# The last pair's up products ahead of the down products of the last pair but one, in two expert stages

## The reference

```python
xn = rms_norm(x)
group = argmax(xn @ w_router_group + b_router_group)
two experts = top_2 of the logits of that group       # weights e_w
for each expert e, on the tokens that chose it:
    hid = silu(xn @ w1[e]) * (xn @ w3[e])             # gate and up: 1024 x 512 each
    y   = hid @ w2[e]                                 # down: 512 x 1024
x = x + sum over a token's two experts of e_w * y
```

## Time and profile before

| | us |
|---|---|
| median of 3 runs | 2242.19 (2239.77 to 2244.62) |
| the profiled execution | 2242.67 |
| its span | 2240.8 |
| TensorE busy | 2118.8 (95%) |
| VectorE busy | 733.4 (33%) |
| ScalarE busy | 387.8 (17%) |
| GpSimd busy | 245.4 (11%) |
| bytes moved | 528.81 MB, mean 236 GB/s |

### The profile page before, as it was taken

How to read it: one execution, slowest core, us unless ns; L and a number is a source line. 1 busy time by engine, 2 the same in 40 slices (tenths; PEclk the granted TensorE clock), 3 DMA queues, 4 the chain that set the end, 5 groups by cost and what they waited for, 6 DMA issues and landing times.

```text
span 2240.8 us, 27584 instructions
## 1 busy us (share of the span) xinstructions
PE 2118.8 (95%) x11803; PEld 1130.3 (50%) x11803; DVE 733.4 (33%) x1742; ACT 387.8 (17%) x742; POOL 245.4 (11%) x258
## 2 busy tenths in 40 slices
PE   9999899999998999989999999999999999998987
PEld 5454666654444433335556568764674533333332
DVE  3126675323001011041277864522232411111104
ACT  4001132121000100011133353210022100000001
POOL 6001211000000000000001142301110010000001
PEclk9999999999999999999998999999999999999999
DMA  8113104259999999995110021124352699999998
GB/s 300 50 38 113 50 26 169 83 208 389 424 422 428 427 421 427 428 391 179 29 30 2 3 77 39 64 87 150 113 225 94 237 421 427 428 428 427 427 425 334
DMA packets 96686, 528.81 MB, mean 236 GB/s; under 512 B 10286, under 2 KB 26339, under 8 KB 69162
## 3 DMA queue, kind: packets, MB, share of 16 engines
q1 hardware_dynamic: 82450, 492.11, 54.1%
q0 software_dynamic: 8160, 17.88, 2.2%
q10 hardware_dynamic: 5944, 16.94, 2.0%
HBM read 509.04 MB, written 30.41 MB: 241 GB/s over the span
## 4 chain that ended last, share of the span: by engine, by line
PE 79%; DMA 11%; DVE 5%; SPq 2%; ACT 1%; issue 1%; POOL 0%; DVEq 0%; POOLq 0%; ACTq 0%
PE ps L204 75%; DMA SC<-in_w_e_up 2%; DMA RING<-in_w_e_up 2%; DMA SC<-in_w_e_down 2%; SPq L1688 2%; DMA SC<-in_w 1%; DMA XT<-in_w 1%; DMA EX<-in_w_e_up 1%; DMA RING<-in_w 1%; PE ps L1774 1%; ACT SC L1931 1%; PE ps L1822 1%; PE ps L3349 0%; PE ps L2754 0%; DVE RING L3420 0%
## 5 line engine op out<-in xcount | busy, mean ns | idle before, releaser
L204 PE MATMUL ps<-SC 64*64 64x64 f32 (+5 forms) x5408 | 743.9, 348 | 46.7 <-ACT SC L1931 11.0
L204 PE MATMUL ps<-RING,SC 128*64 128x512 f32 (+2 forms) x1648 | 558.6, 587 | 22.7 <-ACT SC L1931 5.5
L204 PEld LDWEIGHTS ps<-SC 64*64 64x64 f32 (+2 forms) x5408 | 331.4, 146 | 343.9 <-issue 292.4
L204 PEld LDWEIGHTS ps<-RING,SC 128*64 128x64 f32 (+2 forms) x1648 | 192.6, 151 | 256.1 <-issue 245.5
L204 PE MATMUL ps<-XT,RING 128*128 128x256 f32 (+2 forms) x944 | 317.1, 489 | 3.0 <-DVE XT L200 1.6
L204 PEld LDWEIGHTS ps<-XT,RING 128*128 128x128 f32 (+1 forms) x944 | 176.2, 190 | 115.6 <-issue 100.4
L1999 DVE SCALAR_TENSOR_TENSOR SC<-ps,ST,SC 128x512 f32<-128x512 f32 x30 | 22.5, 751 | 643.2 <-PE ps L204 643.2
L204 PE MATMUL ps<-RING,XT 128*128 128x512 f32 (+1 forms) x384 | 147.8, 545 | 0.0
L204 PE MATMUL ps<-SC,RING 128*128 128x512 f32 (+2 forms) x504 | 134.6, 432 | 2.3 <-DVE SC L1270 0.8
L204 PE MATMUL ps<-XT,SC 128*64 128x512 f32 (+2 forms) x312 | 117.1, 528 | 2.0 <-DMA SC<-in_w_e_up 1.3
L204 PEld LDWEIGHTS ps<-RING,XT 128*128 128x128 f32 x384 | 69.5, 195 | 76.5 <-issue 75.8
(11 more groups left out here) (497 smaller groups left out, 1950.9 us busy)
## 6 DMA issues: line engine op xcount, KB each, us to landing
SC<-in_w SPq DMA_DIRECT2D x48, 2048.0 KB, 29.1
RING<-in_w SPq DMA_DIRECT2D x36, 2048.0 KB, 28.9
RING<-in_w_in SPq DMA_DIRECT2D x15, 2048.0 KB, 9.1
SC<-in_w_e_gate SPq DMA_DIRECT2D x14, 2048.0 KB, 40.9
SC<-in_w_e_up SPq DMA_DIRECT2D x13, 2048.0 KB, 41.7
SC<-in_w_e_down SPq DMA_DIRECT2D x13, 2048.0 KB, 37.5
RING<-in_w_e_gate SPq DMA_DIRECT2D x11, 2048.0 KB, 40.4
RING<-in_w_e_up SPq DMA_DIRECT2D x11, 2048.0 KB, 42.2
```

Of the source, the lines that this page charges most:

```text
L204: return e.matmul(out, l, r, start=st, stop=sp, skip_group_check=True)
```

## The change

SP's order of loads is now: pairs 0 to 13 as they were, gate and up of pair 14, gate and up of pair 15, down of pair 14, down of pair 15. The down weights of pair 14 come as column halves too, and before them SP waits for the first halves of the last gate weights (the two share a semaphore). `down_p` and `down_a` are split into the transposition (`ht_p`, `ht_a`) and the products; for pair 15 the transposition comes first, then pair 14's down products, then pair 15's. ScalarE's copy of HT for pair 15 waits for the end of pair 14's down products. Pair 15's down result goes to XG in place of YS, both halves by ScalarE. VectorE makes the one-hots after the last gate product.

```diff
--- before.py
+++ after.py
@@ -1687,33 +1687,38 @@
                         k = dst.shape[1] // 2
                         e.dma_start(dst[:, k * hf:k * hf + k], src[:, k * hf:k * hf + k]).then_inc(*(up or slots.up)(label))
 
-            put_n = 0
-            while put_n < 6 * NPAIR:
+            turn = list(range(6 * LAST - 2)) + [6 * LAST + i for i in (0, 1, 2, 3, -2, -1, 4, 5)]
+            i_ = 0
+            while i_ < 6 * NPAIR:
+                put_n = turn[i_]
                 if put_n == 2 and bi == 0:
                     mk_s(e)
                 if bi == 0 and put_n in MV_LOADS:
                     mv_s(e, 1 - MV_LOADS.index(put_n))
                 if put_n == nfirst:
                     halves(([c.on("half of w", 0, 0)], None), ([], None))
-                    put_n += 2
+                    i_ += 2
                 elif put_n in (6 * LAST, 6 * LAST + 2):
                     j = put_n // 2 % 3
                     halves(([], lambda label: c.up(f"dh{j}", "half", LAST, j)), ([], None))
-                    put_n += 2
-                elif put_n == 6 * LAST + 4:
+                    i_ += 2
+                elif put_n in (6 * LAST - 2, 6 * LAST + 4):
+                    p_ = put_n // 6
                     loads = [put(n) for n in (put_n, put_n + 1)]
+                    if p_ < LAST:
+                        W.wait_ge(*c.on("half", LAST, 0))
                     for hf in range(2):
                         for label, free, dst, src in loads:
                             for f in () if hf else free:
                                 W.wait_ge(*f)
-                            e.dma_start(dst[:, :, 512 * hf:512 * hf + 512], src[:, :, 512 * hf:512 * hf + 512]).then_inc(*(slots.up(label) if hf else c.up("dh2", "half", LAST, 2)))
-                    put_n += 2
+                            e.dma_start(dst[:, :, 512 * hf:512 * hf + 512], src[:, :, 512 * hf:512 * hf + 512]).then_inc(*(slots.up(label) if hf else c.up("dh2" if p_ == LAST else "dh0", "half", p_, 2)))
+                    i_ += 2
                 else:
                     label, free, dst, src = put(put_n)
                     for f in free:
                         W.wait_ge(*f)
                     e.dma_start(dst, src).then_inc(*slots.up(label))
-                    put_n += 1
+                    i_ += 1
             slots.put(hots_at, ("hot", bi), (c, ("add", NT - 1, 1)))
             for i in ybs:
                 for f in slots.put(i, ("yb", bi, i), (c, ("X", NT - 1)))[1]:
@@ -1814,13 +1819,15 @@
                     i = mm(e, b[:, :], hotp[tt], X[:, tt, 512 * hf:512 * hf + 512], tt == 0, tt == NT - 1)
                 i.then_inc(*c.up("p", "pick", q, hf))
 
-        def down_p(e, f, q, banks, w):
+        def ht_p(e, f, q, banks):
             b, free = banks("ht", q)
             W.wait_ge(*free)
             W.wait_ge(*f.on("hd", q))
             for j in range(4):
                 i = e.transpose(b[:, j * 128:(j + 1) * 128], HD.rearrange("p (c k) -> p k c", k=4)[:, j, :], ident[:, :])
             i.then_inc(*f.up("p", "ht", q))
+
+        def down_p(e, f, q, banks, w):
             W.wait_ge(*f.on("ev", "ht", q))
             for hf in range(2):
                 wv = w(q, 2, hf)
@@ -1841,7 +1848,7 @@
             for tt in range(NT):
                 b, free = c.take("add", tt, hf)
                 W.wait_ge(*free)
-                i = mm(e, b[:, :], hot2[:, tt * 128:(tt + 1) * 128], YS[:, hf * 512:(hf + 1) * 512], True, tt != 3)
+                i = mm(e, b[:, :], hot2[:, tt * 128:(tt + 1) * 128], XG[:, hf * 512:(hf + 1) * 512], True, tt != 3)
                 if tt < 3:
                     i.then_inc(*c.up("p", "add", tt, hf))
             if hf:
@@ -1866,7 +1873,7 @@
             def w(q, j, hf):
 
                 labels = [(f"m{bi}", q, j, x) for x in range(2)]
-                if q == LAST and not hf:
+                if not hf and (q == LAST or (q, j) == (LAST - 1, 2)):
                     W.wait_ge(*c.on("half", q, j))
                 else:
                     for l in labels:
@@ -1886,7 +1893,11 @@
                     for tt in range(NT):
                         i = e.transpose(b[:, tt * 128:(tt + 1) * 128], hot[:, tt * 128:(tt + 1) * 128], ident[:, :])
                     i.then_inc(*c.up("p", "hot T"))
-                down_p(e, c, q, c.take, w)
+                ht_p(e, c, q, c.take)
+                if q == LAST:
+                    down_p(e, c, LAST - 1, c.take, w)
+                if q != LAST - 1:
+                    down_p(e, c, q, c.take, w)
                 if q == 0:
                     turn_e(e, c, 1, c.take)
                 if bi == 0 and q in MV_AFTER:
@@ -1908,6 +1919,7 @@
             def pair_p(q):
                 turn_e(e, o, q, banks)
                 up_p(e, o, q, banks, ow)
+                ht_p(e, o, q, banks)
                 down_p(e, o, q, banks, ow)
 
             segments(e, over(e), pair_p)
@@ -1924,16 +1936,22 @@
                 W.wait_ge(*c.on("rsl"))
                 e.activation(HD, at("up", q, 0)[:, :], AF.Silu, scale=rsl[:, i_:i_ + 1]).then_inc(*f.up("a", "ev", "up", q, 0))
 
-        def down_a(e, f, q, at):
+        def ht_a(e, f, q, at):
             W.wait_ge(*f.on("ht", q))
             if f is c and q == 0:
                 W.wait_ge(*c.on("nov"))
+            if f is c and q == LAST:
+                W.wait_ge(*f.on("down", q - 1, 1))
             e.activation(HT, at("ht", q)[:, :], AF.Copy).then_inc(*f.up("a", "ev", "ht", q))
+
+        def down_a(e, f, q, at):
+            if f is c and q == LAST:
+                for hf in range(2):
+                    W.wait_ge(*f.on("down", q, hf))
+                    e.activation(XG[:, 512 * hf:512 * hf + 512], at("down", q, hf)[:, :], AF.Copy).then_inc(*f.up("a", "ev", "down", q, hf))
+                return
             if q >= 1 and f is c:
                 W.wait_ge(*f.on("y", q - 1))
-            if q == LAST and f is c:
-                W.wait_ge(*f.on("down", q, 0))
-                e.activation(YS[:, 0:512], at("down", q, 0)[:, :], AF.Copy).then_inc(*f.up("a", "ev", "down", q, 0))
             W.wait_ge(*f.on("down", q, 1))
             e.activation(YS[:, 512:1024], at("down", q, 1)[:, :], AF.Copy).then_inc(*f.up("a", "ev", "down", q, 1))
 
@@ -1960,7 +1978,11 @@
                 if q == LAST:
                     W.wait_ge(*c.on("hot T"))
                     e.activation(hot2, c.at("hot")[:, :], AF.Copy).then_inc(*c.up("a", "ev", "hot"))
-                down_a(e, c, q, c.at)
+                ht_a(e, c, q, c.at)
+                if q == LAST:
+                    down_a(e, c, LAST - 1, c.at)
+                if q != LAST - 1:
+                    down_a(e, c, q, c.at)
                 if bi == 0 and q in MV_AFTER:
                     for n in range(4):
                         mv_a(e, c, 1 - MV_AFTER.index(q), n)
@@ -1970,6 +1992,7 @@
 
             def pair_a(q):
                 up_a(e, o, q, fixed_at)
+                ht_a(e, o, q, fixed_at)
                 down_a(e, o, q, fixed_at)
 
             def table():
@@ -2308,9 +2331,11 @@
                 turn_v_(e, c, q + 1, c.at)
                 if q + 2 in picks:
                     hotp_v(e, q + 2)
-                down_v(e, c, q, c.at)
+                if q < LAST - 1:
+                    down_v(e, c, q, c.at)
             hots_v(e)
             up_v(e, c, LAST, c.at)
+            down_v(e, c, LAST - 1, c.at)
             n_over = over(e)
             for kind, tt, hf in (("add", 0, 0), ("add", 1, 0), ("add", 2, 0), ("table", 0, 0), ("table", 1, 0), ("add", 0, 1), ("add", 1, 1),
                                  ("table", 2, 0), ("add", 2, 1), ("add", 3, 0), ("add", 3, 1)):
@@ -2360,7 +2385,7 @@
 
         def hots_v(e):
 
-            W.wait_ge(*c.on("w", LAST - 1, 2))
+            W.wait_ge(*c.on("w", LAST, 0))
             W.wait_ge(*c.last("v"))
             for k, dst in ((0, hot), (1, hot2)):
                 for tt in range(NT):
```

## The result

The changed kernel takes 2250.6 us (median of 10 runs, 2247.2 to 2259.0), the one before 2242.8 beside it. The ratio is 1.0040 with a 95% interval of 1.0029 to 1.0051, which is 9.0 us more (6.5 to 11.4); the two medians as such are 7.8 us apart, inside that interval. A second measurement gave 1.0037 (1.0024 to 1.0050). The forecast was 2254 in a range of 2247 to 2261. The profiled execution took 2252.8 us with a span of 2251.1.

What follows compares the result with a forecast made beforehand. Weight streams bound both expert stages up to the last landing, with a tail behind. Profiled 2242.67 us plus 6.5 (second stage) and 5.5 (first) gave 2254.7, less 0.5 for the median 2254.2, say 2254; range 2247 to 2261.

Steps and rivals of the forecast that it cites:

- Place and sign: Expert stage tails: down 14, scatter, ytab reads and table passes come to stand in series; slower, chance 0.85.
- (c): Stage tails: the reads of ytab are hidden after all and TensorE's tail stays level, 2242 us; chance 0.03.
- (d): TensorE, not the bytes, is the bound and the order cures its stalls: 3.9 us a stage, 2234.5; chance 0.05.
- Loads: Down 14's column halves move at 389 instead of 421 GB/s, +0.8 us; they land at about 2201.4 and 2206.8.
- Scatter: Pair 14's scatter, second stage, starts at 2212.7 after down 14 and ScalarE's copies, takes 7.8 us, lands at 2220.5.
- Rival (a): Without the stream the scatter lands in 4.7 us: +2 to +3.5 us a stage, 2246 to 2249; chance 0.18.
- the row of 512 KB written by ACT: Nearest row without load for the scatter's landing: 3.7 us, with POOL's 1.0 us 4.7 us.
- Reads: Four ytab reads sent at 2220.5 into an empty queue: 4.8 us for the first, 2.5 more for each, to 2232.8.
- The row of memV: The 1024 KB row used to price the first ytab read in an empty queue: 4.8 us.
- Clock: Second stage: after 4.6 us idle TensorE runs its last eight records at half clock, 1.5 us added.
- Sum: Second stage 6.5 us and first stage 5.5 us longer, added to 2242.67 us: 2254.7, by the median 2254.
- ck1's place: First stage: ck1, 2 MiB queued behind the reads, lands at 1009.3; key products +4.2 to +6.5 us, 5.5 taken.

Runs made afterwards that it cites:

- The kernels with the shifted scatter: Two variants of the changed kernel: ScalarE copying YS before HT (2252.3 us, ratio 1.0037), and down 14 loaded whole (2254.5 us, ratio 1.0057).

## Why the prediction was right

- Place and sign: right in each step of the chain. Up 15 landed early, down 14 in its place, the scatter came 18 and 15 us later, the reads followed it into an empty queue, VectorE waited for the first, TensorE for the fourth. The waits were shorter than forecast: 2.70 us for VectorE where it had about 5, 3.09 for TensorE where it had 4 to 5, and 5.4 and 5.1 us from scatter to reads where it had 7 to 9. The run without the scatter shows that the loss hangs on this chain, so rivals (c) and (d) fell; (d) also because TensorE's waits at pair 14's down weights went and brought nothing.
- Loads: the halves of down 14 were forecast 0.8 us late for their narrow pieces. The rate was as forecast (385 to 388 GB/s from 2197 to 2217), yet the second half started 22.9 us after the event where up 15's had started at 22.5 and 23.2. The term isn't seen; the event itself may carry some of it.
- Scatter: it starts at 28.6 where the forecast had 29.8; 1.1 us of this is the second half of down 14, at 22.9 where it had 24.0. **The mis-sized term of the sum is its landing: 7.8 us taken, 5.1 and 5.4 measured**, since the stream ended under it. The kernels with the shifted scatter gave 6.0 and 2.7. Rival (a) had the mechanism, a landing without the stream, but its 4.7 is near the 5.1 and 5.4 by luck: where the engines were idle it took 2.7, and in the changed kernel the stream was still ending.
- The forecast also took the scatter for 512 KB, which is all of YS. The traces show 144 packets and 0.17 MB for it (0.16 MB in the first stage), and 102 of them are under 512 B where it moves alone. `scatter` has a bounds check that drops places without a token; that this is the reason is read from the code. So neither the row of 512 KB written by ACT nor a formula fed with 512 KB was a price for it.
- Reads: the first landed 4.8 us after its issue, as forecast (5.9 in the first stage). The fourth was forecast 12.3 us after the first issue and landed 13.3 us after it (2236.39 less 2223.07); the 11.99 of the chain count from its own issue, 1.3 us later. That SP issues the four one after another was left out. The row of memV was the right one for the first. The fit that the Trainium skill gives for a DMA issued from GpSimd ("DMA: Bandwidth & Descriptors", "Anatomy of one DMA") makes 4.4 us of such a read, an estimate, since SP issued this one; the 4.8 measured are near it. For the scatter with the 0.17 MB that it moved, the same fit of the Trainium skill gives an estimate of 2.4 us, near the 2.7 measured with the engines idle and far from the 5.4 and 7.8 beside the stream.
- Clock: 1.5 us taken, 1.7 measured in the eight records (5.40 against 3.70).
- Sum: 6.5 and 5.5 us taken; 4.2 and 5.1 found from the common event. In the second stage the last add was forecast to end at 55.9 from the event and ended at 53.6: 1.2 us by the earlier scatter and 2.4 by its landing, less 1.0 for the fourth read and about 0.2 for the clock. So the errors offset each other in part. For the first stage ck1's place was named, and the key products came 5.1 us later in place of 5.5; but the kernel with the new order in that stage alone lost 2.7 us, so the time bears out this term less well than the trace.

## What to carry to other kernels

When a step is moved later, follow what its result feeds as well as what it reads: here a scatter that had 1.3 us of cover before SP's next issue lost it by being moved 15 us and more, and two transfers that had cost nothing behind the weights came to stand one after the other with nothing beside them. Two tails in two traces are to be compared from a common event just before them, not by the clock of the trace, and from more than one trace, since here such an event was good to some 1.7 us only. And a gain in a tail counts only if the next stage starts from it; in the first stage here it started from a load further back in the queue.

## What was not expected of the hardware

A scatter's time to landing isn't a constant that can be taken from the nearest row. The same 0.16 to 0.17 MB took 7.8 and 7.9 us inside the stream of weights, 6.0, 5.4 and 5.1 us when the stream ended under it, 2.7 us when it had ended. Where it was issued 0.5 us earlier under the stream's end, the reads behind it began no earlier.

The packets of the scatter's queue show where the time goes. Each of these three windows of the second stage holds all 144 of them: the kernel before, 2200.27 to 2203.87; the changed kernel, 2218.97 to 2222.57; down 14 loaded whole, 2223.23 to 2224.23.

```profile
q0 software_dynamic: 144, 0.17, 13.2%
...
q0 software_dynamic: 144, 0.17, 13.9%
...
q0 software_dynamic: 144, 0.17, 47.1%
```

Counted from the scatter's start that is 4.0 to 7.6 us in the full stream, 1.4 to 5.0 us under its end, and 1.4 to 2.4 us with idle engines. In the full stream the first packets came 2.6 us later than in the idle case; under its end they began as early as in the idle case, but the last of them came 2.6 us later, among the last packets of weights. This looks as if rows wait on each DMA engine behind weights already given to it. The windows tell queues apart and not engines, so this last step is a reading.
